# Rounding ahead of squaring at the launch, and a last sum of squares left to TensorE, in a two-layer streaming encoder step

## What is computed

```
def rmsnorm(x, g):
    xf = x.astype(jnp.float32)
    y = xf * lax.rsqrt(jnp.mean(xf * xf, axis=-1, keepdims=True) + EPS)
    return (y * g).astype(x.dtype)
...
def token_mix(x, pos, P, rg_buf, rg_h, rw_shift, rw_state, past_ckv, past_kr):
    p = rmsnorm(x, P['norm_mix']) @ P['w_in']
...
    return x + y, (rg_buf_new, rg_h_new, rw_shift_new, rw_state_new, ckv, kr)
...
def layer(x, pos, P, rg_buf, rg_h, rw_shift, rw_state, past_ckv, past_kr, mem_k, mem_v):
    x, new_state = token_mix(x, pos, P, rg_buf, rg_h, rw_shift, rw_state, past_ckv, past_kr)
    x = x + mem_attend(rmsnorm(x, P['norm_mem']), mem_k, mem_v, P['mem_w_q'], P['mem_w_o'])
    h = rmsnorm(x, P['norm_ffn'])
    x = x + jnp.square(jax.nn.relu(h @ P['ffn_w1'])) @ P['ffn_w2']
    return x, new_state
```

## Time and profile before

| | |
|---|---|
| median of 3 runs | 1888.54 us (1884.87, 1888.54, 1893.43) |
| the profiled execution | 1883.82 us, of which the span of the instructions is 1882.0 |
| PE busy | 1785.2 us (95% of the span) |
| DVE busy | 1141.3 us (61%) |
| ACT busy | 868.9 us (46%) |
| POOL busy | 256.6 us (14%) |
| transfers | 149.56 MB, mean 79 GB/s |

### The profile page before, as it was taken

One profiled execution on the slowest core, in us unless ns is written; L12 is line 12 of the kernel. 1 busy time (PEld: TensorE's weight loads), 2 busy tenths in 40 slices (PEclk: granted clock), 3 DMA queues, 4 the chain that ended last, 5 costly groups with the idle time before them and its releaser, 6 DMA issues.

```text
span 1882.0 us, 38137 instructions
## 1 busy us (share of the span) xinstructions
PE 1785.2 (95%) x16290; PEld 1652.7 (88%) x16290; DVE 1141.3 (61%) x1977; ACT 868.9 (46%) x1588; POOL 256.6 (14%) x222
## 2 busy tenths in 40 slices
PE   5998988899999999999999999889999999999997
PEld 5985776899889999999999667779987999999996
DVE  6687665454457765666467776655443776655653
ACT  5444545553346544444345355554533664444432
POOL 2020000200012222221100100001000232222201
PEclk9999999999999999999999999999999999999998
DMA  5200001453112222222231000123610312222221
GB/s 224 68 20 1 4 4 41 152 174 129 34 57 79 90 101 99 94 90 92 90 127 57 9 2 3 36 90 131 207 57 12 101 68 98 105 92 100 90 91 59
DMA packets 38760, 149.56 MB, mean 79 GB/s; under 512 B 4416, under 2 KB 4576, under 8 KB 36928
## 3 DMA queue, kind: packets, MB, share of 16 engines
q1 hardware_dynamic: 36288, 131.05, 20.3%
q0 software_dynamic: 2304, 16.06, 2.3%
HBM read 139.68 MB, written 7.41 MB: 78 GB/s over the span
## 4 chain that ended last, share of the span: by engine, by line
PE 79%; DVE 10%; ACT 7%; issue 2%; POOL 1%; DMA 1%; DVEq 0%; ACTq 0%; SPq 0%; POOLq 0%
PE PS L816 57%; PE PS L979 13%; PE PS L1008 5%; PE PS L998 1%; DVE wL L1885 1%; ACT wH L1402 1%; DVE wL L1889 1%; DVE hbL L2358 1%; PE PS L1256 1%; DVE stat L2250 1%; ACT hb L1402 1%; ACT L1402 1%; DVE xT L1915 1%; POOL sq L707 1%; ACT hH L1402 0%
## 5 line engine op out<-in xcount | busy, mean ns | idle before, releaser
L816 PE MATMUL PS<-hH,wH 128*128 128x272 f32 x1760 | 384.7, 300 | 32.7 <-DMA cst<-cst_in 16.1
L1402 ACT ACTIVATE wH<-ring 128x1024 fp32r<-128x1024 f32 (+1 forms) x294 | 261.6, 891 | 329.9 <-PE PS L816 270.3
L816 PE MATMUL PS<-hH,wL 128*128 128x272 f32 x1760 | 367.9, 290 | 0.0
L816 PE MATMUL PS<-hL,wH 128*128 128x272 f32 x1760 | 367.2, 290 | 0.0
L1889 DVE TENSOR_TENSOR wL<-ring,wH 128x1024 fp32r<-128x1024 f32 x182 | 230.7, 1269 | 187.9 <-ACT wH L1402 187.2
L816 PEld LDWEIGHTS PS<-hH,wH 128*128 128x128 f32 x1760 | 280.2, 190 | 48.7 <-issue 17.8
L816 PEld LDWEIGHTS PS<-hH,wL 128*128 128x128 f32 x1760 | 279.7, 190 | 0.0
L816 PEld LDWEIGHTS PS<-hL,wH 128*128 128x128 f32 x1760 | 278.2, 190 | 0.0
L979 PE MATMUL PS<-hbH,wH 128*128 128x272 f32 x784 | 227.1, 290 | 1.2 <-DVE hT L2414 0.9
L979 PE MATMUL PS<-hbH,wL 128*128 128x272 f32 x784 | 227.0, 290 | 0.0
L979 PE MATMUL PS<-hbL,wH 128*128 128x272 f32 x784 | 225.6, 288 | 0.0
(11 more groups left out here) (373 smaller groups left out, 3560.3 us busy)
## 6 DMA issues: line engine op xcount, KB each, us to landing
ring<-wall SPq DMA_DIRECT2D x238, 512.0 KB, 3.3
lw<-lw_in POOLq DMA_DIRECT2D x2, 1856.0 KB, 7.9
xT<-x_in SPq DMA_DIRECT2D x4, 544.0 KB, 6.3
y_out<-hT SPq DMA_DIRECT2D x8, 272.0 KB, 2.1
mem<-mem_in POOLq DMA_DIRECT2D x2, 1024.0 KB, 5.1
mks<-mks_in POOLq DMA_DIRECT2D x2, 1024.0 KB, 6.9
mvs<-mvs_in POOLq DMA_DIRECT2D x2, 1024.0 KB, 9.9
memk_out<-mkp POOLq DMA_DIRECT2D x2, 1024.0 KB, 6.2
```

Of the source, the lines that this page charges most:

```text
L816: return e.matmul(out, lhsT=a, rhs=b, start=start, stop=stop)
L1402: return e.activation(out, in_, f, **kw)
```

## The change

At the launch ScalarE rounds all eight rows first and squares them afterwards; the squares go to buffers of their own (sq[0] and seven rows of oT, which is not in use yet). VectorE adds them up instead of GpSimd. The norm's product moves from behind tile 0 to the inside of tile 1, ahead of its sixth row, and the wait for the constants moves there from ahead of the first matmul; rs is then made in ScalarE's turn for tile 1. SP issues weight tile 2 ahead of the constants, and GpSimd issues the small weights as soon as the constants are there. Two tiny operations for the recurrent mixer move to the front, and ScalarE's first table load no longer stands behind a wait for x. At the end GpSimd's seventh add is gone: TensorE multiplies the sum of the first seven rows and the eighth square by `ones` one after the other into the same PSUM sum (`rms_end`).

```diff
             load(1)
+            load(2)
             e.dma_start(cst[:, :], cst_d).then_inc(cst_ld, 16)
-            for n in range(2, DEPTH * NT):
+            for n in range(3, DEPTH * NT):
                 load(n)
...
-            add_squares(0)
...
+            e.wait_ge(cst_ld, 16)
             load_small(0)
+            e.wait_ge(s["sq_added"], 7)
...
-                add_squares(3 * l + 3, 7, 7)
+                    add_squares(3 * l + 3, 7, 7)
...
+            def rms_end(r):
+
+                e.wait_ge(s["sq_added"], 7 * r + 6)
+                halves(Q(2), ones, sq[:, 0, :], True, False)
+                e.wait_ge(s["sq_ready"], 8 * (r + 1))
+                halves(Q(2), ones, sq[:, 1, :], False, True).then_inc(s["rms_sum"], 1)
...
                 if i == 0:
-                    rms(3 * l)
+                    if l:
+                        rms(3 * l)
...
                     for j in range(8):
+                        if (l, st, i, j) == (0, "in", 1, 5):
+                            e.wait_ge(cst_ld, 16)
+                            rms(0)
...
-            e.wait_ge(cst_ld, 16)
             for l in range(DEPTH):
                 dense(l, "in", h_from=0)
...
-            rms(3 * DEPTH)
+            rms_end(3 * DEPTH)
...
+            e.wait_ge(setup_abs, 1)
+            act(stat[:, 0:4], stat[:, 4:8], ACT.Exp, scale=-1.0).then_inc(setup_exp, 1)
+            split(0)
             e.wait_ge(vec_ld, 16)
             for k in range(8):
                 e.wait_ge(x_ld[k // 2], 16)
-                if k in (1, 7):
-                    split(k // 7)
                 scaled_hi(0, "g_mix", k)
-                square(0, k)
-            e.wait_ge(setup_abs, 1)
-            act(stat[:, 0:4], stat[:, 4:8], ACT.Exp, scale=-1.0).then_inc(setup_exp, 1)
+            split(1)
+            for k in range(8):
+                act(oT[:, k, :] if k else sq[:, 0, :], xT[:, k, :], ACT.Square).then_inc(s["sq_ready"], 1)
...
-                    if i == 0:
+                    if i == 0 and l or i == 1 and not l:
                         rstd(3 * l)
...
-            for k in range(8):
-                if k in (1, 7):
-                    split(k // 7)
-                scaled_lo(0, 0, "g_mix", k)
...
+            split(0)
+            for k in range(8):
+                scaled_lo(0, 0, "g_mix", k)
+            split(1)
+            for k in range(1, 8):
+                e.wait_ge(s["sq_ready"], k + 1)
+                if k > 1:
+                    e.wait_ge(s["sq_added"], k - 1)
+                tt(sq[:, 0, :], sq[:, 0, :], oT[:, k, :], ALU.add).then_inc(s["sq_added"], 1)
             e.wait_ge(setup_exp, 1)
```

## The result

The changed kernel takes 1877.61 us (median of six runs, 1874.79 to 1879.33), the kernel before 1888.91 in the same comparison (six runs, 1884.87 to 1893.68). The ratio is 0.9934, with a 95% interval of 0.9921 to 0.9947: 11.3 us less by the medians, some 10 to 15 us by the interval, so faster by over 0.5%. In this comparison the times of the two don't overlap. The profiled execution took 1877.13 us.

A forecast was written before the change was run, and what follows sets the result against it. The touched bounds lie at the ends: TensorE's start waits (16.1 us constants, 3.0 last remainder, with the square-and-add chain behind) and the final add. 10.0 + 1.8 - 0.5 = 11.3 us off the median 1888.54 gives 1877.2, range 1871 to 1885.

The forecast's parts named there:

- Arrivals, first tile, rounding, split 1: Launch: last x piece lands at 10.7 us, TensorE starts at 8.0, rounding ends at 13.1, VectorE's split 1 at 14.5.
- The adds on VectorE: Launch: seven adds at 0.77 us each, between bounds of 0.73 and 1.34, end at 19.9, or 23.9 by the upper bound.
- The product and rs: Launch: TensorE reaches the norm's product at 19.7, waits 0.2, needs 1.08 us; rs is there at 24.6 to 25.5.
- step 7: ScalarE at launch: split 3 done 20.6 to 21.5, table load 1.28 us, then 2.68 us to rs at 24.6 to 25.5.
- step 8: VectorE at launch: free at 24.3, evacuates tile 0 once rs is there; tile 2 begins at 25.9 instead of 35.86.
- The launch as a whole: From the start to tile 2: a gain of 10.0 us, between 9.5 and 10.5.
- The end: After the last square: the logarithm begins 1.8 us earlier, or 1.5 if the ones product takes 1.63 us again.
- GpSimd's moved instruction: Its ISA instruction now stands ahead of the memory squares' first add: a cost of 0.5 us, bounds 0 and 6.2.
- rival B: At the memory squares, GpSimd's moved instruction takes 8 us or more: gain about 7, 1881.5 us; chance 0.12.
- A: Rival: the clock falls at the new 2.6 us gap ahead of tile 2: gain 9.6, 1878.9 us; chance 0.14.
- C: Rival at launch: VectorE's adds take 1.34 us each or its lead is lost: gain 8.2, 1880.3 us; chance 0.10.
- D: Rival at launch: small weights delay load 3 and evacuations; slower by over 0.5%, about 1898, if landing past 41; chance 0.03.

The follow-up runs named there:

- adds_gpsimd: The changed kernel with the launch's seven adds on GpSimd again, from the eight separate buffers: 1882.85 us, ratio to the kernel before 0.9960.
- end_only: The kernel before with only the new end (seven rows' sum and eighth square multiplied by ones one after the other): 1887.76 us, ratio 1.0002.
- before_again: The kernel before, unchanged, profiled and timed again: 1887.99 us, ratio 0.9985 against itself.
- memory_squares: The changed kernel with the memory tokens' squares also in eight buffers and added by VectorE: 1871.6 us, ratio to the kernel before 0.9916.
- small_weights_first: The changed kernel, but GpSimd issues the small weights at once, without waiting for the constants: 1883.71 us, ratio to the kernel before 0.9959.
- launch_only: The changed kernel with the end of before (GpSimd's seventh add, one ones product): 1881.06 us, ratio to the kernel before 0.9963.
- cst_wait_only: The kernel before with only the wait for the constants moved from ahead of the first matmul to the norm's product: 1891.39 us, ratio 1.0020.

## Why the prediction was right

The forecast of 1877.2 us (1871 to 1885) stands against 1877.61, and the sum of 11.3 against 11.3 by the medians. The mechanism was right: the waits that were to go went, and the one that was to be left is VectorE's. That the two sums agree to 0.1 is luck, since the interval alone spans 10 to 15 us; by the traces the steps make 9.8 + 1.5 to 1.8 - 0, so 11.3 to 11.6. By its steps:

*Arrivals, first tile, rounding, split 1.* TensorE was forecast at 8.0 and started at 8.18; the last remainder was to be done at 13.1 and was at 12.94; split 1 on VectorE at 14.5, here 14.14. TensorE has no wait from 8.18 to the end of tile 1. The squares were sized too long: eight at 0.66 were to end at 18.5, but each starts before the one ahead of it has ended, and ScalarE takes up split 2 at 17.17.

*The adds on VectorE.* The choice between 0.73 and 1.34 was 0.77, nearer to the lower bound since the remainder's slow 1.34 was blamed on GpSimd beside it. It is 0.726 for the instruction and 0.81 per add in the chain (5.70 us for seven), ending at 19.76 where 19.9 was forecast. The remainder's 0.78, eight times out of eight, bears the blame out, and so do VectorE's small operations in adds_gpsimd (4.42 us against 1.14). adds_gpsimd shows what the other choice costs.

*The product and rs.* 19.91 with 1.16 us, forecast 19.9 with 1.08. rs was there at 23.79 instead of 24.6 to 25.5. The squares were done 1.2 us earlier than forecast, and load 3 let ScalarE's split 3 begin at 18.38, where I had it land between 19.0 and 20.4. So the first table load was over before the product was, and the logarithm waited for the product (0.36 us) and not for ScalarE's splits, as step 7 has it. This is the largest miss in the sum. It also changes who comes last: step 8 had VectorE free at 24.3 and waiting for rs, but VectorE's own queue (split 2 done at 24.02) was the later of the two. With it the idle ahead of tile 2 was 1.5 instead of 2.6 us, outside the 2 to 3 us named as a sign, and tile 2 came at 24.86 instead of 25.9. In the other profiles it was 25.10 to 25.83, so the forecast lies at the late edge of what comes out; in three of them TensorE waited 0.6 to 1.2 us for the adds ahead of the product, so the adds have no slack to speak of.

*The launch as a whole.* Forecast 10.0, in the first pair of profiles 11.0. But 1.7 of these were a fall of the clock before tile 2 in the first profile of before. end_only, with the same launch, has such a fall too (0.50 from 26 to 28); before_again has none, and there tile 2 begins at 34.15. Over three executions with the launch of before (35.86, 35.53, 34.15: mean 35.2) and five with the new one (24.86, 25.10, 25.73, 25.55 and 25.83 of memory_squares: mean 25.4) it is 9.8; against before_again alone, 8.7.

*The end.* Forecast 1.8, bound 1.5; the traces show 1.8 against the first profile of before and 1.5 against before_again, whose last product took 1.35 and not 1.63. The table load decides, as forecast, with the product (1.18) just under it.

*GpSimd's moved instruction.* Forecast -0.5 with bounds 0 and 6.2; it cost nothing. GpSimd's first memory add begins after an idle of 5.36 us where the earlier trace rows has 5.35, and takes the same 0.73. So rival B fell, and so did the thought that a first add pays 0.5: in adds_gpsimd too, where GpSimd's first add stands in the launch, none of the seven takes over 1.39 us. The Trainium skill (GPSIMD Engine Reference, section Architecture) has some 6 us for loading code at the first call of a freshly loaded GpSimd kernel. Between the issue of the memory tokens' transfer (324.76) and that add lie 5.9 us, in which nearly all of it could hide, so the trace neither agrees nor disagrees, and no run here shows the load itself.

*The rivals.* A: the granted clock did not fall at the new gap, 1.5 us long (the launch's windows all have 1.00), nor at the gaps of 1.4 to 1.5 us in the four other profiles with this launch. It fell at the old one of 3.0 us in the first profile of before and at 3.3 in end_only, and not at 2.5 in before_again. But the prediction's reason, that a shorter gap is safer, is not shown by that: ahead of the memory product waits of nearly the same length went both ways. In the first profile of before the window behind 3.58 us has 1.00; in the changed kernel the one behind 3.60 us has 0.50:

```profile
340.00:342.00 2.00, 2.00 (x11) 2.00 (x10) 1.52 (x2) 0.45 (x1) 0.00 (x0) 0.50 0.88 287
```

C and D did not happen. What comes near to them was run: slow adds (GpSimd's, 1.47 us each in adds_gpsimd) cost 5 us where C had 3.1, and small weights that meet a wanted transfer (x in small_weights_first, load 3 in D) cost 6 where D had 5.1.

*The sum against the profiled execution.* Here the prediction's working was off by more than its result. It said 1872.5 on the scale of the profile of before, and the changed kernel's profile has 1877.13. Its own condition for being wrong, a middle more than 2 us longer, is met by the pair of profiles (6.1). The cause is the profile of before: its middle was 5.5 us shorter than any other's with the same work, in the main by the granted clock, and it lay 5 us under the median. Since the difference was carried over to the median, the result did not suffer.

What stays open: why launch_only and end_only together show 6.6 us in the times instead of 12.5 (the traces show both parts in full; the clock of launch_only's runs covers some 2 us of it), and what moves the falls of the clock from place to place. Three parts of the launch were not tried alone: the product's place inside tile 1, weight tile 2 ahead of the constants, and the small operations and the table load at the front.

## What to carry to other kernels

Ask of a wait what stands right behind it: the 16.1 us for the constants were worth nothing alone and 8 to 10 us (by medians and by ratios) once the chain behind them was short too. Where two engines hand one buffer back and forth, more buffers and one engine's turn after the other's can take the hand-over off the path, and the same edit paid again at the second place with that pattern, by some 5 us. And before a difference of a few microseconds in the middle of two traces is explained, profile the old kernel a second time.

## What the runs showed of the hardware that was not expected

- The same kernel's middle differs by 6 us between executions (1830.7 and 1836.6 for the kernel before), by falls of the granted clock to 0.50 at changing places.
- A TensorE that gets its rows one by one, with waits of 0.2 to 2.7 us, was at 1.2 GHz from 22 to 30 us (cst_wait_only). It got to the norm's product at 28.17, not earlier than one that had stood still and then ran (27.59).
- At its start TensorE takes 0.66 us for a pair of matmuls and from about 12 us on 0.41 (changed kernel, from 8.18), though the granted clock reads 1.00 in all windows there; in cst_wait_only and adds_gpsimd the reading and the durations go together (0.50, and 2.02 and 2.05 us for the norm's product). The reading alone would hide the slow start.
- Small operations on VectorE beside GpSimd's adds took four times as long (six of 128 x 4: 4.42 us in adds_gpsimd, 1.14 in the changed kernel).
- An add of 128 x 256 on VectorE takes 0.51 us per add in a chain (3.60 us for seven), against 0.81 for 128 x 544 (5.70 for seven): 47% of the columns took 63% of the time.
